# The causal mask of the last two layers' attention, added by VectorE while it takes the row maxima

## The reference, cut to what matters

```python
sc = jnp.einsum('bhqrd,bhkrd->bhrqk', qb, k).astype(jnp.float32) * scale
causal = kpos[None, :] <= qpos[:, None]
p = jax.nn.softmax(jnp.where(causal, sc, -jnp.inf), axis=-1)
a = p[:, :, 0] - lam * p[:, :, 1]
return jnp.einsum('bhqk,bhkd->bhqd', a.astype(v.dtype), v)
```

## Time and profile before

| what | value |
|---|---|
| median of 3 runs | 1877.23 us |
| lowest and highest | 1875.33 and 1878.20 us |
| span of the profiled execution, its own time | 1877.8 us |
| PE busy | 1856.6 us (99%) |
| DVE busy | 1218.2 us (65%) |
| ACT busy | 1070.4 us (57%) |
| mean granted TensorE clock | 0.999 |

### The profile page before, as it was taken

The page is one execution under the profiler, slowest core; times in us unless marked ns, Lnnn a source line. Parts: engine busy times, 40 slices in busy tenths (PEclk is TensorE's granted clock), DMA queues, the critical chain, the costliest instruction groups (busy, mean ns, idle before and its releaser), DMA issues.

```text
span 1877.8 us, 25070 instructions
## 1 busy us (share of the span) xinstructions
PE 1856.6 (99%) x9884; PEld 1576.6 (84%) x9884; DVE 1218.2 (65%) x1796; ACT 1070.4 (57%) x1584; POOL 115.6 (6%) x91
## 2 busy tenths in 40 slices
PE   8999999999999999999999999999999999999999
PEld 6888998788888888899788888888888788888877
DVE  5655696775555555578776555597666568775755
ACT  5444676755444444476766444465776456667642
POOL 0000111100000000011200000002000000110000
PEclk9999999999999999999999999999999999999999
DMA  7555553245555555554224546554345545534553
GB/s 271 184 173 194 169 171 105 87 138 187 183 185 185 187 185 185 178 181 136 92 100 169 188 150 220 171 182 151 131 148 188 176 164 180 168 124 144 182 180 112
DMA packets 88743, 309.86 MB, mean 165 GB/s; under 512 B 9889, under 2 KB 10529, under 8 KB 88625
## 3 DMA queue, kind: packets, MB, share of 16 engines
q1 hardware_dynamic: 87840, 306.35, 48.5%
q0 software_dynamic: 496, 1.65, 0.2%
q10 hardware_dynamic: 288, 0.25, 0.0%
HBM read 307.16 MB, written 1.05 MB: 164 GB/s over the span
## 4 chain that ended last, share of the span: by engine, by line
PE 97%; DVE 1%; ACT 1%; issue 0%; DMA 0%; SPq 0%; POOL 0%; DVEq 0%; ACTq 0%
PE bank L1093 93%; PE bank L1090 4%; DVE WL L1916 0%; DMA RAW<-in_WALL_dram 0%; ACT WH L1483 0%; DVE XC L2064 0%; DVE MO L2234 0%; ACT MPT L1483 0%; DVE STATS L2225 0%; ACT MP L1483 0%; DVE X L2001 0%; ACT XS L1483 0%; SPq L2697 0%; DVE XDD L2271 0%; ACT QTK L1483 0%
## 5 line engine op out<-in xcount | busy, mean ns | idle before, releaser
L1916 DVE TENSOR_TENSOR WL<-RAW,WH 128x1024 fp32r<-128x1024 f32 (+2 forms) x602 | 711.1, 1189 | 462.7 <-ACT WH L1483 458.7
L1483 ACT ACTIVATE WH<-RAW 128x1024 fp32r<-128x1024 f32 (+2 forms) x602 | 614.1, 1029 | 493.6 <-PE bank L1093 484.1
L1093 PE MATMUL bank<-WH,XTH 128*128 128x512 f32 (+2 forms) x1440 | 557.2, 387 | 1.6 <-DVE WL L1916 1.6
L1093 PE MATMUL bank<-WL,XTH 128*128 128x512 f32 (+2 forms) x1440 | 547.8, 380 | 0.0
L1093 PE MATMUL bank<-WH,XTL 128*128 128x512 f32 (+2 forms) x1440 | 547.3, 380 | 0.0
L1093 PE MATMUL bank<-WH,FR 128*128 128x512 f32 x1136 | 351.7, 391 | 0.0
L1093 PEld LDWEIGHTS bank<-WH,XTH 128*128 128x128 f32 x1440 | 271.9, 189 | 51.7 <-DVE WL L1916 2.0
L1093 PEld LDWEIGHTS bank<-WL,XTH 128*128 128x128 f32 x1440 | 271.4, 188 | 51.6
L1093 PEld LDWEIGHTS bank<-WH,XTL 128*128 128x128 f32 x1440 | 272.0, 189 | 50.1 <-issue 1.4
L1093 PEld LDWEIGHTS bank<-WH,FR 128*128 128x128 f32 x1136 | 210.0, 188 | 43.3 <-issue 0.2
L1093 PE MATMUL bank<-WL,FR 128*128 128x512 f32 x568 | 222.1, 391 | 0.0
(11 more groups left out here) (311 smaller groups left out, 1668.3 us busy)
## 6 DMA issues: line engine op xcount, KB each, us to landing
RAW<-in_WALL_dram SPq DMA_DIRECT2D x554, 512.0 KB, 3.3
RAW<-in_WALL_dram SPq DMA_DIRECT2D x38, 256.0 KB, 2.6
RAW<-in_WALL_dram SPq DMA_DIRECT2D x8, 448.0 KB, 3.2
X<-in_x_dram SPq DMA_DIRECT2D x4, 256.0 KB, 4.3
out_dram<-X SPq DMA_DIRECT2D x4, 256.0 KB, 2.0
ROWP<-in_ROWP_dram POOLq DMA_DIRECT2D x1, 672.0 KB, 10.2
CONSTS<-in_CST_dram POOLq DMA_DIRECT2D x1, 664.0 KB, 7.8
ROUNDED<-in_CSTR_dram POOLq DMA_DIRECT2D x1, 208.0 KB, 11.4
```

The costliest lines, as they stand in the source:

```text
L1093: return self.e.matmul(out, lhs, rhs, start=start, stop=stop, skip_group_check=True)
L1483: return self.e.activation(out, in_, func, **k)
L1916: self.e.tensor_tensor(lo, raw, hi.bitcast(F32), ALU.subtract).then_inc(*self.up("lo", j))
```

## The change

In each of the 16 heads (two layers of eight) the two mask products are gone. VectorE instead runs, for each map, one `tensor_tensor_reduce` of 128x128 and one of 128x256: score plus mask, written to `PA` in SBUF, with the row maximum as accumulated output. The mask lies in `MK` (zeros, then the triangle twice; slices of it serve both shapes), in place of constants that nothing read. The exponentials read `PA` and write `PA` in place. The banks of the scores are therefore released by VectorE, no longer by ScalarE. The planner's costs for `as` become P102 V150 A195, and its rule for when the banks become free follows (`FREES`).

```diff
-    mk = np.concatenate([le, np.ones((128, 128), np.float32), le], 1) / np.float32(8)
+    mk = np.concatenate([np.zeros((128, 128), np.float32), neg, neg], 1)
...
-    "as": "P147 V143 A202", "ap": "V125", "at": "P34 A50", "av": "P68 A40",
+    "as": "P102 V150 A195", "ap": "V125", "at": "P34 A50", "av": "P68 A40",
...
+FREES = {"seg": "A", "as": "V"}
...
-            if step[0] == "A":
-                first = first or since
+            if step[0] == FREES.get(name):
+                first = since
         for b in self.next_small(name):
-            self.empty[b] = first if name == "seg" else since
+            self.empty[b] = first or since
...
-        ps = [self.tbank(("as", i, h, r), "as_act", (i, h, r))[1] for r in range(2)]
+        ps = [self.tbank(("as", i, h, r), "as_dve", (i, h, r))[1] for r in range(2)]
...
-                self.mm(ps[r][:, c0:c1], k.QT2[rr, h, q0:q0 + 128], k.QT2[rr, 8 + h, 0:k1], c0 == 0, False)
-        for r in range(2):
-            self.mm(ps[r][:, :].rearrange("p (a s) -> p a s", a=2)[:, :, 0:128], k.EYER, k.CUT[:, 1:2, :].to_broadcast([128, 2, 128]),
-                    False, True).then_inc(*self.up("as_pe", (i, h, r)))
+                m = self.mm(ps[r][:, c0:c1], k.QT2[rr, h, q0:q0 + 128], k.QT2[rr, 8 + h, 0:k1], c0 == 0, c0 > 0)
+                if c0:
+                    m.then_inc(*self.up("as_pe", (i, h, r)))
...
-        if h >= 2:
-            w.wait_ge(*self.at("ap_dve", (i, h - 2)))
...
-                m = self.act(k.PA[:, h % 2, r, c0:c1], k.PS[k.bank["as", i, h, r]][:, c0:c1], ACT.Exp, bias=mx[:, 2 * r + t:2 * r + t + 1],
+                m = self.act(k.PA[:, h % 2, r, c0:c1], k.PA[:, h % 2, r, c0:c1], ACT.Exp, bias=mx[:, 2 * r + t:2 * r + t + 1],
...
-            e.tensor_reduce(mx[:, 3 * r:3 * r + 3], k.PS[k.bank["as", i, h, r]][:, 0:384].rearrange("p (r k) -> p r k", r=3), AX.X,
-                            ALU.max).then_inc(*self.up("as_dve"))
-        w.wait_ge(*self.now("as_dve"))
-        e.tensor_tensor(m3[:, :, 1], m3[:, :, 1], m3[:, :, 2], ALU.max).then_inc(*self.up("as_dve"))
+            for t, c0, c1 in ((0, 0, 128), (1, 128, 384)):
+                m = e.tensor_tensor_reduce(k.PA[:, h % 2, r, c0:c1], k.PS[k.bank["as", i, h, r]][:, c0:c1],
+                                           k.MK[:, 128 - 128 * t:256], 1.0, -3e38, ALU.add, ALU.max,
+                                           accum_out=mx[:, 2 * r + t:2 * r + t + 1])
+            m.then_inc(*self.up("as_dve", (i, h, r)))
```

More of the change, by code:

```diff
@@ L148 @@
     matmul = transpose = activation = tensor_tensor = tensor_scalar = scalar_tensor_tensor = op
-    tensor_copy = tensor_reduce = reciprocal = memset = tensor_tensor_scan = dma_start = op
+    tensor_copy = tensor_reduce = tensor_tensor_reduce = reciprocal = memset = tensor_tensor_scan = dma_start = op
 class Lin:
@@ L1427, in as_ @@
         k, w = self.k, self.w
-        ps = [self.tbank(("as", i, h, r), "as_act", (i, h, r))[1] for r in range(2)]
+        ps = [self.tbank(("as", i, h, r), "as_dve", (i, h, r))[1] for r in range(2)]
         for j in range(2):
             w.wait_ge(*self.at("qkf_act", (i, j, h // 2 * 2)))
-        w.wait_ge(*self.at("const5", 0))
         for c0, c1, q0, k1 in ((0, 128, 0, 128), (128, 384, 128, 256)):
@@ L2507, in as_ @@
         k, w, e = self.k, self.w, self.e
-        mx, neg = k.stat(("asm", i, h % 2), 6), k.stat(("asn", i, h), 4)
-        m3 = mx.rearrange("p (r k) -> p r k", r=2)
+        mx, neg = k.stat(("asm", i, h % 2), 4), k.stat(("asn", i, h), 4)
         scq = k.stat(("scq", i, h // 4), 16).rearrange("p (t g) -> p g t", t=2)[:, 2 * (h % 4):2 * (h % 4) + 2, :]
+        w.wait_ge(*self.at("const6", 0))
         for r in range(2):
             w.wait_ge(*self.at("as_pe", (i, h, r)))
-            e.tensor_reduce(mx[:, 3 * r:3 * r + 3], k.PS[k.bank["as", i, h, r]][:, 0:384].rearrange("p (r k) -> p r k", r=3), AX.X,
-                            ALU.max).then_inc(*self.up("as_dve"))
-        w.wait_ge(*self.now("as_dve"))
-        e.tensor_tensor(m3[:, :, 1], m3[:, :, 1], m3[:, :, 2], ALU.max).then_inc(*self.up("as_dve"))
+            for t, c0, c1 in ((0, 0, 128), (1, 128, 384)):
[3 more added lines that the diff above has]
+            m.then_inc(*self.up("as_dve", (i, h, r)))
         w.wait_ge(*self.now("as_dve"))
         w.wait_ge(*self.at("hq_dve", (i, 0, h // 4)))
-        e.scalar_tensor_tensor(neg.rearrange("p (r t) -> p r t", r=2), m3[:, :, 0:2], -1.0, scq, ALU.mult, ALU.mult).then_inc(
-            *self.up("as_dve", (i, h)))
+        e.scalar_tensor_tensor(neg.rearrange("p (r t) -> p r t", r=2), mx.rearrange("p (r t) -> p r t", r=2), -1.0, scq, ALU.mult,
+                               ALU.mult).then_inc(*self.up("as_dve", (i, h)))
     def ap(self, i, h):
```

## The result

| | median | lowest to highest | runs |
|---|---|---|---|
| before | 1877.72 us | 1875.33 to 1879.56 | 4 |
| after | 1896.48 us | 1893.67 to 1897.11 | 4 |

The ratio is 1.0098, with a 95% interval of 1.0087 to 1.0110: slower, by 18.8 us where 10.7 were forecast, and 3 us above the upper end of the range. The profiled execution of the changed kernel took 1893.67 us (span 1891.9) with a mean granted clock of 0.995. It is the fastest of the four; the other three have 0.992 and 0.993 and spans of 1894.3 to 1895.3. So the trace shows less of the loss than the median does.

What follows compares the result with a forecast made beforehand. TensorE was taken to bound the kernel. Per layer -3.7 + 7.45 + 0.4 + 1.2 = +5.35 us, +10.7 for two layers over a median of 1877.2, gave 1887.9 us; range 1880 to 1893.5 us.

Steps and rivals of the forecast that it cites:

- gain of the removal and of fewer groups: TensorE, per layer: removed mask products save 3.3 us, fewer groups of small work 0.4; together 3.7.
- long piece, less its 3.35 us of work: Between blocks 440 and 441: block 441 starts 10.8 us later, so TensorE stands for 7.45 us per layer.
- wait ahead of `as` 4: TensorE waits 0.4 us per layer for copies of `qkf` and `av` 0, arriving at 26.2 against 26.6 us.
- clock: Behind the long piece, TensorE's granted clock falls to 0.50 in both layers: 1.2 us per layer, bounds 0 and 3.4.
- D: VectorE's time per head to the negative maxima with the new instructions: 1.7 us, within 1.4 to about 2.4.
- my walk: ScalarE's and VectorE's steps added in order from the end of block 440: block 441 starts at 10.8 us.
- the rival of dear instructions: VectorE's new instructions at D = 2.3 cost 2 us more per layer: 1892, or 1895 with longer clock spell; chance 0.12.
- The rival that the gain arrives: ScalarE's chain to the `bo` eviction is short enough that block 441 starts on time: 1869.8 us; chance 0.10.
- The rival of more overlap: Engines overlap more: half of the 7.45 us wait and no clock fall, 1877 to 1880 us; chance 0.08.
- points 1, 3 (6.3 us), 4 and 5: Signs: no mask products, single `as` 0.86 us; TensorE gaps 6 to 9 us; clock 0.50; nothing moved before first `as`.
- 2: Sign in the changed profile: VectorE's ISA instructions appear, and D lies between 1.5 and 2.0 us.

Runs made afterwards that it cites:

- experiment 3: Changed kernel plus products on a constant, results unused, ahead of `at` 6, `av` 6, `at` 7 and block 441: 1887.31 us, ratio 1.0055.
- experiment 4: Changed kernel plus 13 products on a constant, results unused, ahead of block 441 alone: 1891.45 us, ratio 1.0077.
- experiment 2: Kernel before, mask products kept, with the changed kernel's planner numbers and rule for free banks: 1898.58 us, ratio 1.0113.
- experiment 7: Changed kernel with planner head starts of the hybrid layers altered, `diff_head` 150 to -50 and `evicted` -50 to 300: 1871.70 us, ratio 0.9967.
- 9: Kernel before, mask products kept, in the order with `diff_head` -50 and `evicted` 300: 1876.89 us, ratio 1.0000.
- 10: Changed kernel with `diff_head` -50 and `evicted` 300, measured once more beside the run with mask products: 1871.52 us, ratio 0.9969.
- experiment 8: Changed kernel with only the planner's `evicted` altered in the hybrid layers, from -50 to 400: 1877.41 us, ratio 1.0000.
- experiment 1: Changed kernel's instructions in the order of the kernel before (old planner costs for `as`, old bank rule): 1875.83 us, ratio 0.9992.
- experiment 5: Changed kernel with the first `bo` eviction of each hybrid layer moved ahead of `as` 4: 1894.16 us, ratio 1.0088.

## Why the prediction was wrong

The direction, the place and the chain of waits were right; the size was short, and the clock's part in the chain was missing. Per layer, against before, with the measured values of the profiled execution (the gain by difference: 41.05 + 11.22 + 21.89 - 69.33 = 4.83 is what a layer loses without the clock's fall, its last stretch taken from experiment 3):

| term | forecast | measured |
|---|---|---|
| gain of the removal and of fewer groups | -3.7 | -3.0 |
| long piece, less its 3.35 us of work | +7.45 | +7.87 |
| wait ahead of `as` 4 | +0.4 | 0 |
| clock | +1.2 | +4.5 (layer 1), +1.4 (layer 2) |
| sum | +5.35 | +9.35 (layer 1), +6.19 (layer 2) |

- **The step that failed is the clock.** "1.2 us per layer, bounds 0 and 3.4". Experiment 3 prices it at 5 us per layer, 10.1 for both where the sum had 2.4; this alone is nearly the whole of the 8.1 us between forecast and median. I had priced it from one spell of 3.4 us over full blocks. Two things were wrong in that. In layer 1 the clock stayed down from 1374 to 1387.4, four times as long as the spell I had taken; that the waits and small products which went on there held it down is likely, though only experiment 4 speaks for it. And I priced only the blocks: the small products of the long piece run slower too, and they lie in the chain that ends with the eviction, since ScalarE waits for them (0.85, 0.26 and 0.86 us in the rows of layer 1 above), so the piece grew from 11.22 to 12.94 us. The 4.5 us of layer 1 are 1.7 for that and 2.8 for the blocks behind. Layer 2 of the profiled execution was close to my figure (1.4), as the clock fell only at the very end of the long piece (0.98 over it). The other three runs have a lower mean clock (0.992 and 0.993), and experiment 2's layers both had 10 us or more, so this was probably the exception.
- **The long piece** was sized well: 11.22 us for 10.8. Some luck is in that. D was 0.3 us too long, which hid that VectorE started 0.19 us later than I had it (1.37 us in, for 1.18) and a part of the 0.47 us by which ScalarE's two copies behind splits came late. The `bo` eviction started 10.38 us in (10.1 by my walk), and block 441 another 0.84 later (0.75).
- **The gain was overrated** by 0.7 us per layer. The pairs and singles came as read. By the starts, the scores of a layer now take 6.64 us (one pair, six single heads) instead of 9.87, which is 3.2 saved, against 3.3 forecast. Of the 0.4 us for fewer groups nothing came: by the starts, the 18 blocks take 50.05 us before and 50.03 in experiment 3. A block starts slower behind `at` and `av` (0.31 us to its second product), but not behind masks: the earlier trace rows has 1331.68 to 1331.91 there, 0.23. Of the 12 groups before, 4 ended with masks; all 8 that are left end with something else. So there was nothing to save. And an `av` directly behind scores now costs 0.1 us more. "That is the whole possible gain", 7.4 us, is 5.4 to 5.9 us in truth (experiments 7, 9 and 10).
- **VectorE.** D is 1.40 us, not 1.7, so that the wait ahead of `as` 4 did not come. The lower bound, 1.4, was the truth, and with it the walk itself had no wait there. I gave the accumulator reads a price, and they run beside the next instruction. So the rival of dear instructions fell too. The exponentials took 2.13 us (2.1).
- **The rival that the gain arrives** fell because the chain was what I had read. But its premise, an order in which TensorE starts on time, exists: experiment 7, which comes 2 us short of its figure. The rival of more overlap fell as well: the wait was 7.87 us, not half of 7.45.
- **What would show it:** points 1, 3 (6.3 us), 4 and 5 came, the last in the order of work, with a start that varies by some 3 us from run to run; 2 did not (1.40 against 1.5 to 2.0).

What stays open: when the clock falls and for how long in a given execution. The same piece of work left it at 0.50 for some 3 us in one layer and for over 13 in the other, and the median differs from the profiled run by 2.8 us. Also, the median of before holds now and then a clock spell elsewhere, so the 10.1 us are uncertain by one to two.

## What to carry to other kernels

Taking work from the engine that bounds the kernel pays only if the order of the work lets that engine arrive earlier everywhere. Here the same edit gave +18.8, -0.4, -1.7 and -5.9 us under four orders (the planner's own, experiments 8, 1 and 7), so an edit that changes a planner's costs has to be tried with the planner's old numbers and with a few neighbours too. And where several short waits of TensorE come close together, price the clock as well: once for the blocks behind, and once more for the small products inside the chain.

## What was not expected of the hardware

- Waits of 1.8 and 1.3 us within 6 us of small work brought the granted clock to 0.50 in each profiled layer of experiment 4, though TensorE was busy for 2.73 of the 5.30 us ahead (layer 1). It is no rule: in layer 2 of the changed kernel the clock stayed at 1.00 over the same waits and fell only in the next long one, at 1725.6. Waits of 0.86 and 0.67 us (experiment 8), a single 1.00 (experiment 1) or a single 1.79 (experiment 5) did not bring it down.
- Products whose result nobody reads made the kernel 9.2 us faster (experiment 3), by keeping the clock at 1.00.
- The accumulator read of VectorE is listed with 0.08 us and starts together with the next instruction: 0.22 and 0.34 us from start to start for adding a mask to 128x128 and 128x256 scores in PSUM, writing them to SBUF and taking the row maxima.
